# 129 products of constants on the tensor engine of a decoder step, and adaLN rounds of the attention at other units

## What is computed

```
mod = silu(c) @ ada_w[layer] + ada_b[layer]        # sh1, sc1, g1, sh2, sc2, g2 for each of 9 conditions
h   = rms_norm(x) * (1 + sc1) + sh1
x   = x + g1 * mixer(h)      # layer 0: sliding window attention; layer 1: gated linear attention (GLA)
h   = rms_norm(x) * (1 + sc2) + sh2
x   = x + g2 * moe(h)        # 64 experts of width 256, top 8 of 4 groups, and one shared expert
...
y   = rms_norm(x)            # after layer 1; the caches and the GLA states are outputs too
```

## Time and profile before

| | |
|---|---|
| median of three timed runs | 1622.3 us |
| profiled execution, its own time | 1629.76 us |
| its span, first to last instruction | 1628.0 us |
| busy: PE, DVE, ACT | 93%, 25%, 21% |
| mean granted clock of the tensor engine | 0.954 of full |
| read from HBM, mean rate | 499 MB, 313 GB/s |

### The profile page before, as it was taken

The page is one execution under the profiler, slowest core; times in us unless marked ns, Lnnn a source line. Parts: engine busy times, 40 slices in busy tenths (PEclk is TensorE's granted clock), DMA queues, the critical chain, the costliest instruction groups (busy, mean ns, idle before and its releaser), DMA issues.

```text
span 1628.0 us, 21788 instructions
## 1 busy us (share of the span) xinstructions
PE 1510.0 (93%) x8868; PEld 804.4 (49%) x8868; DVE 414.3 (25%) x996; ACT 345.4 (21%) x921; POOL 49.2 (3%) x86
## 2 busy tenths in 40 slices
PE   5997997999999999999899989799999999999995
PEld 2444664545455445454355445454444545445543
DVE  1116515212212112221153233421111211122113
ACT  2114413111111111111253222401111111111112
POOL 0000201000000000000010010100000000000000
PEclk7998989999999999999989998999999999999996
DMA  9867423899999989999952252188999998999981
GB/s 394 344 262 310 165 75 122 359 384 365 421 421 415 378 340 421 422 413 374 376 218 103 104 192 82 56 359 316 352 422 420 418 372 343 423 421 407 377 342 33
DMA packets 65892, 509.64 MB, mean 313 GB/s; under 512 B 7776, under 2 KB 8048, under 8 KB 10208
## 3 DMA queue, kind: packets, MB, share of 16 engines
q1 hardware_dynamic: 62064, 490.17, 74.5%
q0 software_dynamic: 3728, 18.07, 3.0%
HBM read 499.16 MB, written 11.01 MB: 313 GB/s over the span
## 4 chain that ended last, share of the span: by engine, by line
PE 82%; DMA 8%; ACT 3%; DVE 3%; issue 2%; SPq 1%; ACTq 0%; DVEq 0%
PE bank L1765 24%; PE banks L1793 11%; PE banks L1709 8%; DMA s_gu_ring<-in_moe_wu_dram 8%; PE banks L421 5%; PE banks L1018 3%; PE ybank L1730 3%; PE banks L641 3%; PE bank L1733 3%; PE banks L1730 3%; PE bank L475 2%; PE banks L1046 2%; PE banks L1555 1%; PE bank L1718 1%; PE bank L487 1%
## 5 line engine op out<-in xcount | busy, mean ns | idle before, releaser
L1765 PE MATMUL bank<-s_gu_ring,s_hbuf 128*32 128x512 f32 (+1 forms) x2560 | 420.0, 610 | 26.0 <-DMA s_gu_ring<-in_moe_wu_dram 24.3
L1765 PEld LDWEIGHTS bank<-s_gu_ring,s_hbuf 128*32 128x32 f32 (+1 forms) x2560 | 134.1, 125 | 302.7 <-issue 302.7
L1793 PE MATMUL banks<-s_dn_ring,s_hTs 128*32 128x512 f32 (+1 forms) x1280 | 211.6, 597 | 2.0 <-ACT s_wsl L1819 2.0
L1709 PEld LDWEIGHTS banks<-s_sel,s_htok 128*128 128x128 f32 x1200 | 146.2, 191 | 48.2 <-issue 48.2
L1891 DVE TENSOR_TENSOR s_ylo<-banks,s_yhi 128x512 fp32r<-128x512 f32 x116 | 80.3, 692 | 322.4 <-ACT s_yhi L1839 322.4
L1709 PE MATMUL banks<-s_sel,s_htok 128*128 128x256 f32 (+1 forms) x1200 | 158.1, 287 | 0.5 <-issue 0.5
L1839 ACT CAST s_yhi<-banks 128x512 fp32r<-128x512 f32 x116 | 68.0, 586 | 296.3 <-PE banks L1793 296.3
L1883 DVE SCALAR_TENSOR_TENSOR s_hh<-s_sg,s_wsl,bank 128x256 f32<-128x256 f32 x58 | 27.9, 481 | 388.8 <-ACT s_sg L1829 388.8
L1793 PEld LDWEIGHTS banks<-s_dn_ring,s_hTs 128*32 128x32 f32 (+1 forms) x1280 | 58.8, 122 | 123.1 <-issue 120.9
L1829 ACT ACTIVATE s_sg<-bank 128x256 f32<-128x256 f32 x58 | 22.3, 385 | 404.3 <-PE bank L1765 404.3
L1018 PE MATMUL banks<-s_gu_ring,s_hbuf 128*128 128x512 f32 x128 | 55.9, 593 | 0.5 <-DVE s_rs L1302 0.5
(11 more groups left out here) (410 smaller groups left out, 1541.8 us busy)
## 6 DMA issues: line engine op xcount, KB each, us to landing
s_gu_ring<-in_moe_wg_dram SPq DMA_DIRECT2D x128, 1024.0 KB, 10.2
s_gu_ring<-in_moe_wu_dram SPq DMA_DIRECT2D x128, 1024.0 KB, 12.2
s_dn_ring<-in_moe_wd_dram SPq DMA_DIRECT2D x128, 1024.0 KB, 11.8
s_gu_ring<-in_ada_w_dram SPq DMA_DIRECT2D x24, 2048.0 KB, 9.5
s_gu_ring<-in_win_dram SPq DMA_DIRECT2D x6, 2048.0 KB, 12.4
s_gu_ring<-in_wqkv_dram SPq DMA_DIRECT2D x3, 2048.0 KB, 16.4
s_gu_ring<-in_wo_dram SPq DMA_DIRECT2D x2, 2048.0 KB, 7.7
s_gu_ring<-in_shared_up_dram SPq DMA_DIRECT2D x2, 2048.0 KB, 11.9
```

What stands on the lines that cost most here:

```text
L1709: last = pe.matmul(b[:, 256 * (m % 2):256 * (m % 2) + width], w[:, m * P:(m + 1) * P], sel[q % 2][:, s, 0:width], start=(n == 0), stop=(n ...
L1765: last = pe.matmul(W0[o:o + n, :], xg4[:, p % 3, k, o:o + n], w[:, k, :, :], start=(k == 0), stop=(k == KC - 1))
L1793: last = pe.matmul((W1, W2)[half][o:o + n, :], hTs[:, f, o:o + n], dn_ring[:, dn_of[(l, r)][0], w0:w0 + 512], start=(f == 0), stop=(f == 1))
```

## The change

A new function issues n products of two constants, the identity as weights and 128 columns of ones as the moving operand, into a bank that nothing reads at that time. It is called at ten places of the program text (some run for both layers): in the front's rounds 0 to 3 (3 after each part, 7 after each fold, 5 after the last), in the attention at unit 3 (5), in the router between the two waits (20, in both layers), at the end of each MoE before the wait for `y_low` (10) and after the last `combine` (8), and after the folds of `next_norm` (10). That is 129 products, or 258 records. Rounds 12 and 13 move from units 0 and 4 to 2 and 5.

```diff
+        def keep_awake(pe, b, n):
+
+            for _ in range(n):
+                pe.matmul(b[:, 0:P], ident, ones, start=True, stop=True)
+
...
                 AT_SLOT[-1] = 11
-                for n in range(12, 18):
-                    AT_SLOT[4 * (n - 12)] = n
+                for n, i in zip(range(12, 18), (2, 5, 8, 12, 16, 20)):
+                    AT_SLOT[i] = n
...
                     for n in range(4):
                         ada_part(pe, n)
+                        keep_awake(pe, bank[6], 3)
                         ada_fold(pe, n)
+                        keep_awake(pe, bank[6], 7 if n < 3 else 5)
...
                         if i - 1 in AT_SLOT:
                             ada_fold(pe, AT_SLOT[i - 1])
+                        if i == 3:
+                            keep_awake(pe, bank[6], 5)
...
                         pe.wait_ge(S["tok_hi"], 6 * l + 6)
+                        keep_awake(pe, W0, 20)
                         pe.wait_ge(S["topk_full"], l + 1)
...
                             last.then_inc(S["y_full"], 1)
+                    keep_awake(pe, W0, 10)
                     pe.wait_ge(S["y_low"], 2 * (l + 1) * NP)
                     rest_pe(pe)
                     combine(NP - 1).then_inc(S["acc_full"], 1)
+                    keep_awake(pe, W0, 8)
...
                 for n in ada_pair(i):
                     ada_fold(pe, n)
+                keep_awake(pe, W0, 10)
```

## The result

The changed kernel takes 1605.3 us (median of six runs, 1597.72 to 1607.51) against 1622.06 us (six runs, 1615.47 to 1633.79) for the kernel before. The ratio is 0.9874, with a 95% interval from 0.9842 to 0.9905: 1.3% faster. The forecast was 1611 us, 0.7% faster, within 1600 to 1622.

A forecast was written before the change was run, and what follows sets the result against it. PE, busy 93% of the span with about 150 us at the low clock, was taken as the bound; -7.8 + 2.5 - 0.7 - 1.5 - 2.5 - 5.3 = -15.3 us from 1629.8 gave 1614.5, adjusted to 1611 us, range 1600 to 1622.

The forecast's parts named there:

- The front: Rounds 0 to 3 at the high clock, period 5.3 us against 6.63, projection near 38.2 instead of 43.42: -7.8 us.
- Rival (b): In the front, saturated transfers swallow the gain: of 7.8 us 2 remain, total 1617; chance 0.16.
- The attention: Moved rounds 12 and 13: PE waits about 4.6 us before round 12's fold, clock falls; +2.5 us, worst 4.5.
- The routers: 20 products delay the top 8 by 0.7 us, later products run faster: -0.7 layer 0, -1.5 (capped) layer 1.
- The end of the first MoE and the norm: Products there lie in waits at no cost; less PE time at the low clock: -2.5 us in layer 0.
- The end of layer 1: Last combine gains 1.5 us and `final` 3.8 if transposes hold the high clock: -5.3 us.
- Rival (a): In `final` and `next_norm` the clock falls once only transposes run: 3.8 to 4.8 us missing, 1615; chance 0.22.
- Rival (c): At all places, products of identity and ones do not hold the clock: +28 us, 1650, slower by 1.7%; chance 0.08.
- three falls of the clock more or fewer inside the passes: Inside the MoE passes: such a change in the number of clock falls would show the prediction wrong.
- half of the 7.5 us: Whole kernel: timed median lies 7.5 us below the profiled run; half taken off, as some recovered falls are absent there.

The follow-up runs named there:

- second comparison: The changed kernel run once more, unchanged, beside the kernel before: ratio 0.9896 [0.9856, 0.9936].

## Why the prediction was right, and where it was not

**The size.** Measured is a gain of 1.3%, and 1.0% in the second comparison, for a forecast of 0.7%. I gave faster by over 1% a chance of 0.31 and within 1% one of 0.61: the less likely side came, near the border.

**The front, right where the clock was low.** The clock is 1.00 in the window; period 5.27 us for 5.3, projection at 38.33 for 38.2, -7.46 us for -7.8. Rival (b) is refuted: the third group of the projection (L648 at 57.40 in after) doesn't wait, and the front alone gives 7.5 us in the timed runs, at least 3 by its interval, where (b) left 2. What the step lacked is that the low front is not in every execution.

**The attention, the step that failed.** The wait before the fold came as described (4.26 us for 4.6, low clock from 127.3 to 134.1). But the cost is about 5 us by the profiles (means of 86.4 and 81.0), not 2.5, and even above my bound of 4.5. What I missed was the other end of the move: I wrote that part 13 "comes a unit later" and asked only when it would bring the clock back, not which wait it had covered. The trace had it: in the kernel before, L661 follows the part of round 13 that ends at once.

```profile
144.35 1.09 PE L661 MATMUL ybank<-s_cst,s_qkv 128*128 128x128 f32 x8
```

The run that moves round 13 alone shows 1.30 us of bare wait and the low clock behind it, and 5.5 us more of attention; it was made with the wait at unit 3 filled.

**The routers: layer 0 right in the first pair, layer 1 mis-sized.** -1.10 us for -0.7, and -2.92 for -1.5. A product costs 4.73 / 20 = 0.237 us, as taken (0.24). L1564 before and L1574 after are the same line: 4.1 us behind the last copy before, 4.6 after, a delay of 0.5 us for 0.7. This is the stretch behind the last copy in layer 0 of after, which answers to the earlier trace rows:

```profile
258.80 4.73 PE L407 MATMUL bank<-s_cst 128*128 128x128 f32 x40 [1.25 <-ACT s_htok L1621]
...
263.37 0.19 PE L1574 MATMUL bank<-s_mb,s_upper_b 128*128 128x64 bf16 x1
...
264.28 1.34 PE L1564 MATMUL banks<-s_hbuf,s_gu_ring 128*128 128x320 f32 x4
```

The products of the shared expert take 1.34 us instead of 2.50. In layer 1 I had worked out 2.4 and capped it at 1.5, since the transfers would not come earlier; in the run with 40 products a later start moved the end by as much, which speaks against the cap, and 2.4 would have been nearer. For the price, the Trainium skill (TensorE: Matmul & The Clock Gate, section Back-to-back issue gap) gives about 81 ns for a pair of load and product; here a record takes 4.73 / 40 = 118 ns, in another number format, and the measurement decides.

**The end of the first MoE and the norm, right in the first pair by luck.** -2.57 us for -2.5, but over all profiles the gain is 4.3 (next table). Where the clock stayed up through the whole stretch, in seven of the ten profiles with products there, it took 38.3 to 38.5 us; in after it still fell once, from 803.1 to 806.5. The term of 2.5 was too small.

**The end of layer 1, right.** -5.55 for -5.3. This is PE's timeline of after there:

```profile
1579.49 0.62 PE L1743 MATMUL bank<-s_ylo,s_gt 128*128 128x512 f32 x2
1579.95 1.95 PE L407 MATMUL bank<-s_cst 128*128 128x128 f32 x16
1582.28 1.21 PE L1933 MATMUL bank<-s_cst,s_hbuf 128*128 128x128 f32 x6 [0.39 <-ACT s_hbuf L1913]
...
1586.21 0.58 PE L1933 MATMUL bank<-s_cst,s_hbuf 128*128 128x128 f32 x3
```

Three transposes take 0.58 us and a chunk comes every 0.97 us (1584.28 to 1588.15 are four), as forecast. This stretch took 24.3 to 24.6 us in all eleven profiles with products there and 28.7 to 30.1 in the three without. Rival (a) is refuted twice: by `final`, where the clock stays at 1.00 though PE only transposes, and by the kernel with transposes at every place. The Trainium skill says in TensorE: Matmul & The Clock Gate, section Part 4: PE-mode transpose, that the full clock doesn't engage for transposes, which don't count as busy in the same way. In this kernel they hold it, by the clock of 1.00 in the front and a ratio of 0.9902 beside 0.9896; that they would raise it from the low level no run shows, and in `final` before they did not (10.76 us of them in 11.30, clock 0.50).

**Rival (c)**, that such products do not hold the clock, is refuted for 128 columns. The narrow ones show that its mechanism exists: slower by 0.65%.

**All profiles, cut alike.** These are means and ranges over the profiles of kernels without and with products at the place (us). The narrow products are left out, and so are the kernels with 17 and 40 products in the two router rows.

| stretch | without | with | difference | predicted |
|---|---|---|---|---|
| start to first scores | 123.0 (3: 118.7 to 126.0) | 119.1 (10: 118.5 to 120.2) | -3.9 | -7.8 |
| attention (with: new units and five) | 81.0 (4: 80.3 to 82.3) | 86.4 (5: 82.9 to 87.8) | +5.4 | +2.5 |
| router to first pass, layer 0 | 54.2 (3: 53.5 to 55.4) | 52.4 (8: 52.3 to 52.5) | -1.8 | -0.7 |
| last pass to the gates of layer 1 | 43.0 (3: 42.0 to 43.6) | 38.8 (10: 38.3 to 39.8) | -4.3 | -2.5 |
| router to first pass, layer 1 | 55.1 (3: 55.0 to 55.3) | 52.4 (8: 52.2 to 52.4) | -2.7 | -1.5 |
| last pass to PE's last record | 29.2 (3: 28.7 to 30.1) | 24.5 (10: 24.3 to 24.6) | -4.7 | -5.3 |
| passes, both layers | 972.1 (3: 968.9 to 976.6) | 968.1 (10: 960.7 to 978.2) | -4.0 | 0 |

The places together come to -12.0, with the passes to -16.0. Three profiles are few: two of those without products in the front had it low for about 20 us or more, one did not, and the row moves by 4 us with that.

**The passes, no effect shown.** Over 14 profiles of 12 programs the passes of layer 0 range from 480 to 491 us, those of layer 1 likewise; the kernel before had 488.36 and 485.34 in its two, the changed one 482.93 and 481.75. The 6.4 us of the first pair lie within this scatter. A gain of a few us there is neither shown nor excluded. As a sign of being wrong I had named three falls of the clock more or fewer inside the passes: the kernel before has six and two in its two profiles, the changed one four and one, so the sign can't serve. Of the sum, the places alone came to -18.8 us for -15.3 in the first pair; with the attention at its usual cost it is about -14. It is near the forecast because misses point opposite ways, the attention against the routers and the norm. The timed gain is about 18 us; the four between the two stay open.

**From profile to median.** I took half of the 7.5 us off. The timed difference was 16.8 us in the first comparison and 19.3 in the second, about 18 together, so the 15.3 subtracted whole from the median, 1607, would have been nearer.

## What to carry to other kernels

A tensor engine that is always busy can still be paid at half speed: look for stretches of low clock, and fill the wait ahead of each with work on constants that ends just before the wait does. Here products of 128 columns did it at 118 ns a record, and products of 32 did not in the front and the router; in the routers the excess over the wait went one for one to the end. When a piece of work is moved, ask of its old place which wait it had covered, besides what it delays at its new one. And cut several profiles of one program at the same landmarks before a difference of a few microseconds is given to a change.

## What the runs showed of the hardware

- Transposes of ones in the waits kept the granted clock at 1.00 from 20.9 to 48.2 us in their one profile, as products did in nine.
- Products of 32 columns with PE busy 27.14 of 27.30 us ran with a mean granted clock of 0.75. They cost as much as wide ones at the high clock: 20 narrow records took 2.42 us (0.121 each), 40 wide ones 4.73 (0.118 each).
- Where the clock falls differs between executions of one program: the front of the kernel before was low for 27.3 us in one profile and for 3.4 in another, and the spans were 1628.0 and 1611.1 us.
